# Shift and scale of the first norm made feature tile by feature tile with the weights stationary, and the first projection chunk woven between them

## The reference

```
m = silu(cond) @ w_ada[l] + b_ada[l]          # cond: c for latents, c_ctx for context; 6 x 1024 columns
shift_a, scale_a, gate_a, shift_f, scale_f, gate_f = split(m, 6)
h = rms_norm(x, norm_mix_g) * (1 + scale_a) + shift_a
z = h @ w_in                                   # 1024 x 1824
```

## Time and profile before

| | us |
|---|---|
| median of 3 runs | 1700.51 (1699.59 to 1705.67) |
| the profiled execution's own time | 1701.98 |
| its span, first to last instruction | 1700.2 |
| PE busy | 1631.1 (96%) |
| DVE busy | 1310.9 (77%) |
| ACT busy | 781.5 (46%) |
| mean granted TensorE clock | 0.985 of full speed |

### The profile page before, as it was taken

One profiled execution on the slowest core, in us unless ns is written; L12 is line 12 of the kernel. 1 busy time (PEld: TensorE's weight loads), 2 busy tenths in 40 slices (PEclk: granted clock), 3 DMA queues, 4 the chain that ended last, 5 costly groups with the idle time before them and its releaser, 6 DMA issues.

```text
span 1700.2 us, 28338 instructions
## 1 busy us (share of the span) xinstructions
PE 1631.1 (96%) x10942; PEld 1560.1 (92%) x10942; DVE 1310.9 (77%) x2309; ACT 781.5 (46%) x1489; POOL 398.5 (23%) x438
## 2 busy tenths in 40 slices
PE   6999989999999999999999989999999999999997
PEld 2998878889999999999999977888999999999997
DVE  5897788877988888888869877887387777677764
ACT  3534767852633333333352476687363333333332
POOL 0033554310012221212114073632001221121111
PEclk8999999999999999999989999999999999999998
DMA  9562000065177777777537310001606666666651
GB/s 369 193 229 65 10 3 1 1 218 167 40 181 193 207 202 191 188 192 195 161 131 241 118 45 1 3 1 39 198 1 156 178 148 162 153 175 166 154 129 62
DMA packets 114138, 223.79 MB, mean 132 GB/s; under 512 B 7488, under 2 KB 39040, under 8 KB 113024
## 3 DMA queue, kind: packets, MB, share of 16 engines
q1 hardware_dynamic: 90800, 177.90, 30.5%
q0 software_dynamic: 22240, 44.14, 15.6%
q10 hardware_dynamic: 1008, 0.61, 0.1%
HBM read 218.01 MB, written 3.57 MB: 130 GB/s over the span
## 4 chain that ended last, share of the span: by engine, by line
PE 84%; DVE 8%; ACT 3%; issue 2%; DMA 1%; POOL 1%; SPq 1%; POOLq 0%; DVEq 0%; ACTq 0%
PE ps L773 24%; PE ps L775 24%; PE ps L774 24%; DVE ps L1672 3%; PE ps L1041 3%; PE ps L1011 1%; PE ps L781 1%; PE ps L1013 1%; PE ps L858 1%; PE ps L816 1%; DMA ada_n<-in_w_ada_first 1%; DVE hT L1657 1%; DVE negmax L1909 1%; PE ps L914 1%; PE ps L796 1%
## 5 line engine op out<-in xcount | busy, mean ns | idle before, releaser
L773 PE MATMUL ps<-act,dhi 128*128 128x320 f32 x704 | 217.8, 309 | 0.0
L775 PE MATMUL ps<-act,dlo 128*128 128x320 f32 x704 | 217.5, 309 | 0.0
L774 PE MATMUL ps<-act,dhi 128*128 128x320 f32 x704 | 217.5, 309 | 0.0
L2036 DVE SCALAR_TENSOR_TENSOR x<-ps,mod,x 128x512 f32<-128x512 f32 x352 | 170.4, 542 | 42.4 <-PE ps L775 42.4
L773 PE MATMUL ps<-hS,whi 128*128 128x320 f32 x640 | 197.8, 309 | 0.0
L774 PE MATMUL ps<-hS,whi 128*128 128x320 f32 x640 | 197.8, 309 | 0.0
L775 PE MATMUL ps<-hS,wlo 128*128 128x320 f32 x640 | 197.8, 309 | 0.0
L1657 DVE TENSOR_TENSOR wlo<-wraw,whi 128x1024 fp32r<-128x1024 f32 (+3 forms) x166 | 192.0, 1166 | 5.1 <-POOL wraw L2296 5.1
L773 PE MATMUL ps<-hT,whi 128*128 128x320 f32 x608 | 188.0, 309 | 2.2 <-DVE hT L1657 2.2
L775 PE MATMUL ps<-hT,wlo 128*128 128x320 f32 x608 | 187.9, 309 | 0.0
L774 PE MATMUL ps<-hT,whi 128*128 128x320 f32 x608 | 187.9, 309 | 0.0
(11 more groups left out here) (265 smaller groups left out, 4331.3 us busy)
## 6 DMA issues: line engine op xcount, KB each, us to landing
ada_w<-in_w_adaT SPq DMA_DIRECT2D x65, 512.0 KB, 5.1
draw<-in_w_down SPq DMA_DIRECT2D x22, 1024.0 KB, 6.0
wraw<-in_up_q SPq DMA_DIRECT2D x22, 768.0 KB, 6.6
wraw<-in_gate_q SPq DMA_DIRECT2D x20, 768.0 KB, 4.4
wraw<-in_gate_q POOLq DMA_DIRECT2D x20, 768.0 KB, 7.2
wraw<-in_up_q POOLq DMA_DIRECT2D x20, 768.0 KB, 7.1
wi_raw<-in_w_in SPq DMA_DIRECT2D x12, 1216.0 KB, 6.9
wraw<-in_gate_q SPq DMA_DIRECT2D x20, 512.0 KB, 3.4
```

The source lines that it names most:

```text
L773: pe.matmul(dst, lh, rh, start=start, stop=False, skip_group_check=True)
L774: pe.matmul(dst, lh, rl, start=False, stop=False, skip_group_check=True)
L775: return pe.matmul(dst, ll, rh, start=False, stop=stop, skip_group_check=True)
L2036: i = ve.scalar_tensor_tensor(out=x[:, o, c0:c1], in0=y[:, 512 - HALF + c0:512 - HALF + c1], scalar=mod[:, l, 5 * KD + o, q:q + 1], in1=x[ ...
```

## The change

In layer 0 only, all 16 tiles of the first norm's shift and scale are made on TensorE in eight pairs, pair k being shift tile k and scale tile 8 + k. The weights are now the stationary operand and the condition (2 columns) the moving one, so that a result lands as a column at once: 16 float32 matmuls per pair, in `first_ada(k)`. VectorE adds the bias and makes coefficient k (`first_mod(k)`), two small instructions per pair. The rows, their copies and `rows_to_columns` go, and so do the six tiles on VectorE and the transfer of the spread condition; `silu_c` is now made by `spread_silu` (16 matmuls of the broadcast condition against `ident`) and four ScalarE copies. 16 `keep_warm` matmuls follow it.

TensorE's order becomes: `spread_silu`, `keep_warm`, pair 0, `token_sums`, `spread_rstd`, pairs 1 and 2, then part k of chunk 0 (15 matmuls) followed by pair k + 3, for k = 0 to 4, then parts 5, 6 and 7. The spread reciprocal is copied to SBUF by ScalarE. The weights of chunk 0 are split in two halves. The pairs have four slots of 1024 KB: the load of pair k (k >= 4) waits on SP for pair k - 4. x is loaded first, then pair 0, the first chunk of `w_in`, pairs 1 to 7. `REST_AT` of layer 0 gives the first of its chunks four tiles and the last five.

```diff
-RING1, RING2 = 8, 3
-BY_PE = 10
-FIRST = list(range(BY_PE, ADA1))
+RING2 = 3
+SLOTS = 4
-REST_AT = [0, 0, 5, 10, 15, 20, 24]
+REST_AT = [[0, 0, 4, 9, 14, 19, 24], [0, 0, 5, 10, 15, 20, 24]]
+FIRST_BANK = [5, 3, 5, 7, 5, 7, 5, 7]
...
+                    def first_load(k):
+                        if k >= SLOTS:
+                            sp.wait_ge(ada_n_ps, k - SLOTS + 1)
+                        sp.dma_start(first_w(k), a["w_ada_first"][k]).then_inc(ada_n_in[k % SLOTS], 16)
+
+                    sp.dma_start(silu_k[:], a["condT"]).then_inc(cond_k_in, 16)
+                    sp.dma_start(ident[:], a["ident"]).then_inc(ident_in, 16)
+                    for i in range(2):
                         sp.dma_start(x[:, 4 * i:4 * i + 4, :], a["x"][4 * i * P:4 * (i + 1) * P, :]
                                      .rearrange("(k p) n -> p k n", p=P)).then_inc(x_in[i], 16)
+                    first_load(0)
                     wi_load(l, 0)
+                    for k in range(1, KD):
+                        first_load(k)
...
+            def spread_silu():
+                pe.wait_ge(silu_k_done, 1)
+                pe.wait_ge(ident_in, 16)
+                for q in range(2):
+                    for k in range(KD):
+                        m = pe.matmul(ps[:, 2 * q + k // 4, (k % 4) * P:(k % 4 + 1) * P], silu_k[:, k, q:q + 1].broadcast_to([P, P]),
+                                      ident[:], start=True, stop=True, skip_group_check=True)
+                    m.then_inc(silu_ps, 1)
+            def first_ada(k):
+                pe.wait_ge(ada_n_in[k % SLOTS], 16 * (k // SLOTS + 1))
+                if k == 1:
+                    pe.wait_ge(silu_done, 1)
+                if k == 3:
+                    pe.wait_ge(rstd_copied, 1)
+                if k >= 2:
+                    pe.wait_ge(mod_done, k - 1)
+                for half in range(2):
+                    for j in range(KD):
+                        m = pe.matmul(ps[:, FIRST_BANK[k], 2 * half:2 * half + 2], first_w(k)[:, j, half * P:(half + 1) * P],
+                                      silu_k[:, j], start=j == 0, stop=j == KD - 1, skip_group_check=True)
                 m.then_inc(ada_n_ps, 1)
...
                 if l == 0:
-                    pe.wait_ge(silu_k_done, 1)
-                    for pair in range(3):
-                        ada_rows(pair)
+                    spread_silu()
+                    keep_warm(4, ident[:], 16)
+                    first_ada(0)
                     pe.wait_ge(acc_first, KD - 1)
                     token_sums(0, rstd, True, True).then_inc(ss_done, 1)
-                    ada_rows(3)
-                    pe.wait_ge(const_in, 16 * 5)
-                    for pair in range(3):
-                        rows_to_columns(pair)
                     spread_rstd(0)
-                    ada_rows(4)
-                    for pair in range(3, 5):
-                        rows_to_columns(pair)
+                    first_ada(1)
+                    first_ada(2)
+                    pe.wait_ge(wi_half_ready, 1)
+                    pe.wait_ge(mod_done, 2)
+                    for k in range(KD):
+                        if k == KD // 2:
+                            pe.wait_ge(wi_ready, 1)
+                        first_chunk(l, k)
+                        if k + 3 < KD:
+                            first_ada(k + 3)
...
+                    for i in range(4):
+                        sc.wait_ge(silu_ps, i // 2 + 1)
+                        j = sc.activation(silu_c[:, i // 2, (i % 2) * 512:(i % 2 + 1) * 512], ps[:, i, :], ACT.Copy)
+                    j.then_inc(silu_done, 1)
...
+                    for k in range(KD):
                         first_square(k)
+                    sc.wait_ge(wi_in[0], 16)
+                    sc.activation(wi[:, 0, 0, 0:KD // 2], wi_raw[:, 0, 0:KD // 2], ACT.Copy).then_inc(wi_half_hi, 1)
                     rms(0)
+                    sc.activation(wi[:, 0, 0, KD // 2:], wi_raw[:, 0, KD // 2:], ACT.Copy).then_inc(wi_hi, 1)
+                    sc.wait_ge(rstd_ready, 1)
+                    sc.activation(rstd[:], flat(6)[:, 0:T], ACT.Copy).then_inc(rstd_copied, 1)
...
+            def first_mod(k):
+                ve.wait_ge(ada_n_ps, k + 1)
+                ve.tensor_tensor(mod[:, 0, k:ADA1:KD, :], ps[:, FIRST_BANK[k], 0:4].rearrange("p (t q) -> p t q", q=2),
+                                 b_ada[:, 0, k:ADA1:KD].unsqueeze(2).broadcast_to([P, 2, 2]), ALU.add).then_inc(mod_done, 1)
+                ve.wait_ge(mod_done, k + 1)
+                ve.scalar_tensor_tensor(out=coef[:, 0, k], in0=mod[:, 0, KD + k, :], scalar=1.0,
+                                        in1=norm_g[:, 0, 0, k:k + 1].broadcast_to([P, 2]),
+                                        op0=ALU.add, op1=ALU.mult).then_inc(coef_k, 1)
```

More of the change, by code:

```diff
@@ L60 @@
 AHEAD = [NEXT[2 * b - 2 + sum(t < b for t in THREE):2 * b + sum(t <= b for t in THREE)] if b else [] for b in range(FB)]
-ORDER = [list(range(BY_PE, NADA)), NEXT + REST]
+ORDER = [list(range(ADA1, NADA)), NEXT + REST]
 HF_DVE = (0, 4, 7)
@@ L380, in build @@
         silu_k_done = sem("silu_k_done")
-        ada_n_in = [sem(f"ada_n_in{i}") for i in range(BY_PE // 2)]
-        rows_ps = sem("rows_ps")
-        rows_done = sem("rows_done")
+        ident_in = sem("ident_in")
+        silu_ps = sem("silu_ps")
+        ada_n_in = [sem(f"ada_n_in{i}") for i in range(SLOTS)]
+        mod_done = sem("mod_done")
+        coef_k = sem("coef_k")
+        rstd_copied = sem("rstd_copied")
+        wi_half_hi = sem("wi_half_hi")
+        wi_half_ready = sem("wi_half_ready")
         acc_first = sem("acc_first")
@@ L386, in build @@
         silu_done = sem("silu_done")
-        ada_in = [sem(f"ada_in{i}") for i in range(RING1)]
+        ada_in = [sem(f"ada_in{i}") for i in range(5)]
         ada_done = sem("ada_done")
@@ L524, in ring_of @@
                 return 2, NEXT.index(t)
-            return (RING2, t - ADA1) if t in REST else (RING1, t - BY_PE)
+            return RING2, t - ADA1
         def ada_slot(l, t):
             slot = slot_of(l, t)
-            if l == 0 and t >= GATE[0] and slot >= 6:
-                where = ada_g[:, slot - 6]
-            elif slot < 2:
+            if slot < 2:
                 where = ada_w[:, slot]
@@ L699, in _ @@
                         sp.dma_start(wq_raw[:], a["w_q_up"][l].rearrange("(k p) n -> p k n", p=P)).then_inc(wq_in, 16)
-                    for t in REST[REST_AT[c]:REST_AT[c + 1]]:
+                    for t in REST[REST_AT[l][c]:REST_AT[l][c + 1]]:
                         ada_load(l, t)
@@ L906, in queries @@
                 m.then_inc(qm_ps, 1)
[L908 to L923, removed]
-                m.then_inc(ada_n_ps, 1)
+            def spread_silu():
[6 more added lines that the diff above has]
+                    m.then_inc(silu_ps, 1)
@@ L926, in _, with first_chunk @@
+            def first_chunk(l, k):
+                pe.wait_ge(h_ready, l * 2 * KD + k + 1)
+                for t in range(NT):
+                    m = split_mm(ps[:, t, 0:ICW], hT[:, k, 0, t * P:(t + 1) * P], hT[:, k, 1, t * P:(t + 1) * P],
+                                 wi[:, 0, 0, k, :], wi[:, 0, 1, k, :], k == 0, k == KD - 1)
+                    if k == KD - 1:
+                        m.then_inc(z_ps, 1)
             pe.wait_ge(ones_set, 1)
@@ new lines, in first_modulated, with low, wi_half @@
+            def first_modulated():
+                def low(k):
+                    if k in HF_DVE:
+                        ve.wait_ge(hf_dve, sum(j <= k for j in HF_DVE))
+                    ve.wait_ge(h_hi, k + 1)
+                    lo(hT[:, k, 1], hf[:, k % 2], hT[:, k, 0]).then_inc(h_ready, 1)
+                def wi_half(part, done):
+                    lo(wi[:, 0, 1, part], wi_raw[:, 0, part], wi[:, 0, 0, part]).then_inc(done, 1)
+                for k in range(1, KD):
+                    ve.wait_ge(sq_ready, k + 1)
+                    if k == 1:
+                        ve.tensor_tensor(rstd[:], sq[:, 0], sq[:, 1], ALU.add).then_inc(acc_first, 1)
+                    else:
+                        ve.wait_ge(acc_first, k - 1)
+                        ve.tensor_tensor(rstd[:], rstd[:], sq[:, k % 2], ALU.add).then_inc(acc_first, 1)
+                ve.wait_ge(const_in, 16 * 4)
+                first_mod(0)
+                inverse(0)
+                for k in range(KD + 1):
+                    if k == 0:
+                        ve.wait_ge(rstd_copied, 1)
+                    if k == 1:
+                        low(0)
+                    if k < KD:
+                        if k >= 2:
+                            ve.wait_ge(h_hi, k - 1)
+                        ve.tensor_tensor(tn[:, k % 2], x[:, k], rstd[:], ALU.mult).then_inc(tn_ready, 1)
+                        if k in HF_DVE:
+                            ve.wait_ge(tn_ready, k + 1)
+                            if k >= 2:
+                                ve.wait_ge(h_ready, k - 1)
```

(23 more changed lines are left out.)

105 lines of the change are left out of this document (33 added, 72 removed).

## The result

The changed kernel takes 1725.34 us (median), the kernel before 1700.73 beside it: a ratio of 1.0138 (95% interval 1.0125 to 1.0150). That is 24.6 us slower by the medians and 23.5 by the ratio. The forecast was 1727, range 1712 to 1736.

The account below looks back on a forecast made before the run. TensorE, busy 96% of the span, was taken as the bound. Chunk 0 ending at 92.9 instead of 66.8 us adds 26 to 1701.98, giving 1728; the median, 1.5 lower, gives 1727, range 1712 to 1736.

Parts of the forecast that it names:

- The clock: TensorE in the opening: two-column matmuls don't hold the full clock; granted clock near 0.5 from about 18 to 90 us.
- The start: Opening up to pairs 1 and 2: token sums 19.0 to 21.1 us, norm spread to 24.1, these pairs to 37.3.
- Price of a pass: Float32 passes in `first_ada`: 0.205 us each at the half clock, 6.6 per pair; 0.12 at the full clock, 3.8.
- Rises: Returns to full clock in parts 0 to 4 of chunk 0: two taken, 4.8 us less, ending chunk 0 at 92.9.
- Behind chunk 0: TensorE after chunk 0: the same lengths as before, with a cost of 0 to 1 us at the last of `c_norm`.
- The held clock: Rival for the opening: pairs keep the full clock, chunk 0 ends at 66.9 us, no change, time 1702; chance 0.11.
- Cheap pairs: Rival for `first_ada`: 0.07 us per pass, 2.2 per pair, chunk 0 11 us sooner, time 1691; chance 0.04.
- Late transfers: Rival for the opening's loads: transfers arrive too late; excluded unless the rate halves, no chance given.
- Half and half: Rival for chunk 0: clock rises in nearly every part, lasts half of each pair; +8 to +18, about 1714; chance 0.12.
- the main case: Pairs in the opening mostly at the half clock: chunk 0 ends 26 us later, own range 1718 to 1734; chance 0.73.

Follow-up runs that it names:

- `ahead`: The changed kernel with all eight two-column pairs ahead of chunk 0, not woven into it: 1725.83 us, ratio 1.0150 to the kernel before.
- `nowarm`: The changed kernel without the 16 `keep_warm` matmuls: 1729.13 us, ratio 1.0166 to the kernel before.
- `wide128`: The changed kernel with each matmul of a pair streaming 128 columns instead of 2: 1702.95 us, ratio 1.0011 to the kernel before.
- `hybrid2`: `hybrid` with VectorE's four tiles one turn earlier and their loads one place earlier: 1694.18 us, ratio 0.9961 to the kernel before.
- `again`: The changed kernel unaltered, run once more for an undisturbed profile: 1725.96 us, ratio 1.0142 to the kernel before.
- `hybrid`: `wide_sq` with pairs 6 and 7 (four tiles) made on VectorE instead of TensorE: 1697.71 us, ratio 0.9967 to the kernel before.
- `wide_sq`: `wide128` with ScalarE's squares of x ahead of its four copies of the spread condition: 1700.20 us, ratio 0.9991 to the kernel before.

## Why the prediction was right

**The clock.** Right, and it is nearly the whole effect: with two columns the half clock for most of the time from the token sums on, with 128 the full clock, 23.0 us between them. The row that foretold it is 862.2 to 866.7 in the earlier trace rows. Against drops of throughput the Trainium skill (TensorE: Matmul & The Clock Gate, Why this matters for your kernels) asks that there be no idle gaps between bursts of matmuls. Keeping to that was not enough here: `ahead` has 47.7 us without a gap, at 0.50.

**The start.** Token sums forecast 19.0 to 21.1, measured from 18.89; norm spread at 24.1, measured 24.06; pairs 1 and 2 to 37.3, measured 37.6. x came nearly as worked out (7.7 and some 11.4 us, forecast 7.5 and 10.8), the first pair's weights at 13.9 and not 13.4. The 64 passes ahead of pair 0 ended at 12.9 and not at 14, which gained nothing, since pair 0 waited for its weights and the token sums for the adds.

**Price of a pass.** 0.205 us at the half clock was a little low: 6.82 / 32 = 0.213, 0.3 us a pair and 1.2 over the four slow pairs behind the norm. At the full clock 0.12 was right within 3% (3.73 / 32 = 0.117). The Trainium skill (TensorE: Matmul & The Clock Gate, LDWEIGHTS) has a weight load at its columns over 1.2, in ns, which is 107 for 128 columns, with no term for the clock; here the pass takes 117 ns at one level and 213 at the other.

**Rises.** The term that was mis-sized. I took two rises worth 2.4 us each; there were three, and they save 3.0, 2.9 and 2.6 (3.79, 3.90 and 4.25 us against 6.82), and a little in the tails of the parts. That is 3.7 us more than the 4.8 of the sum, less 1.2 for the pass: 2.5 of the 2.7 by which chunk 0 ended sooner than forecast (the marker less 3.3 us is 90.2, I had 92.9). Nothing in the rows of before told how many parts would get a rise. In `nowarm` there are three as well, but behind parts 1, 2 and 3 and not 0, 1 and 2. So the forecast rested on the price of the half clock, and that it came within 2 us of the median is in part luck: chunk 0 ended 2.7 us sooner than forecast, and what arises behind it was not in the sum.

**Behind chunk 0.** No change forecast and none in TensorE's waits to 260 us. The profiled span is 25.5 us longer and the marker 23.3 later; 1.3 of the 2.2 are the last norm's token sums (rows above), 0.9 arise between the second and the third norm. The medians are 24.2 apart.

**The rivals.** The held clock would have given 1702; it is what `wide128` made real, at 1702.95. Its sum (66.9 for the end of chunk 0) came out at 67.2. Cheap pairs: excluded, no float32 pass in any of the profiles read goes below 0.115 us on average. Late transfers: the only wait for a pair's weights is the 1.05 us ahead of pair 0. Half and half: the rows lie between it and the main case, since in three turns of five the pair ran at the full clock nearly to its end. Its own sum was off: 12 to 15 us less than 92.9 is +11 to +14 against 66.8, not +8 to +18.

**What the change gives up even at the full clock.** It makes the norm early and keeps VectorE free, but TensorE bounds this stretch behind the norm (no wait from 24.06 on), and the change hands TensorE all sixteen tiles. Taking four back (`hybrid2`) is what gains.

## What to carry to other kernels

Before matmuls with a full weight load and few moving columns are placed between dense ones, look in the trace at what the granted clock does behind such a stretch; busy TensorE and busy weight loads didn't keep it here. If they must be there, widening the moving operand by a broadcast to 128 columns cost nothing here and held the clock; other widths weren't run. And where TensorE was never idle, weaving moved nothing on balance: count its work at the clock that it will have, and give some of it to an engine that is idle in the same turns, with the handed-over piece placed where that engine waits and not ahead of what TensorE waits for.

## What the runs showed of the hardware that I had not expected

A float32 pass with a 128 x 128 weight load takes 0.117 us with 2 moving columns and with 128 (3.73 us for 32 in `again` and `wide128`), so the step from 2 to 128 columns was free. One idle wait of 2.4 us in `hybrid` was followed within two matmuls by 13 at the half clock. Much shorter ones did it too around the two-column token sums: with idle time of 1.1 and 0.6 us in `wide128` pairs 1 and 2 took 8.73 us, with 0.6 and 0.6 us behind them in `hybrid` 9.04, with 0.6 and 0.2 in `wide_sq` 7.41. And in the 47.7 us of `ahead` matmuls of two columns never got the full clock back, where the wide ones of `wide128` had it back before 26 us.
